# Latent attention: three rounded products of leads and rests for the projections and scores of three head pairs, and key scales spread by two

## The reference, cut to what matters

```python
def mla(c_q, c_kv, k_rope, ...):                       # 8 heads of 64 + 32 dimensions
    q = (rms_norm(c_q, q_a_g) @ w_uq).reshape(B, L, MLA_HEADS, QK_DIM)
    kv = (rms_norm(c_kv, kv_a_g) @ w_ukv).reshape(B, L, MLA_HEADS, NOPE_DIM + V_DIM)
    k = jnp.concatenate([k_nope, k_r], axis=-1)
    q = rms_norm(q, q_norm_g); k = rms_norm(k, k_norm_g)
    ...                                                # rotation of the last 32 dimensions
    o = causal_block_attention(q, k, v)                # softmax(q k^T * scale), causal, times v
    return o.reshape(B, L, MLA_HEADS * V_DIM) @ w_proj
```

## Time and profile before

| | |
|---|---|
| median of 3 runs | 2690.19 us (2686.73 to 2700.15) |
| profiled execution | 2695.79 us, of it span 2693.9 us |
| granted TensorE clock, mean | 0.987 |
| PE busy | 2615.2 us (97%) |
| DVE, ACT, POOL busy | 59%, 41%, 39% |

### The profile page before, as it was taken

One profiled execution on the slowest core, in us unless ns is written; L12 is line 12 of the kernel. 1 busy time (PEld: TensorE's weight loads), 2 busy tenths in 40 slices (PEclk: granted clock), 3 DMA queues, 4 the chain that ended last, 5 costly groups with the idle time before them and its releaser, 6 DMA issues.

```text
span 2693.9 us, 44428 instructions
## 1 busy us (share of the span) xinstructions
PE 2615.2 (97%) x16872; PEld 2318.6 (86%) x16872; DVE 1582.4 (59%) x2486; ACT 1101.7 (41%) x1841; POOL 1052.8 (39%) x675
## 2 busy tenths in 40 slices
PE   7998999999899999999999999999999999999998
PEld 5787788888699998888999999989987777788898
DVE  5665323324489885444476664599884453676665
ACT  4445423323432433433345543323324343454554
POOL 2121444444534222112456544443321124565564
PEclk9999999999999999989999999999999999999999
DMA  5221233232222111101322321222111112332222
GB/s 154 69 80 35 90 101 97 94 93 93 79 72 92 61 58 59 38 26 54 126 87 95 110 95 52 91 92 79 57 55 57 32 40 79 125 104 94 93 102 87
DMA packets 61761, 215.31 MB, mean 80 GB/s; under 512 B 8144, under 2 KB 8144, under 8 KB 61584
## 3 DMA queue, kind: packets, MB, share of 16 engines
q1 hardware_dynamic: 48128, 169.43, 19.8%
q10 hardware_dynamic: 13088, 42.18, 4.7%
q0 software_dynamic: 368, 1.23, 0.2%
HBM read 210.65 MB, written 2.16 MB: 79 GB/s over the span
## 4 chain that ended last, share of the span: by engine, by line
PE 62%; issue 11%; DVE 10%; POOL 5%; POOLq 5%; DVEq 4%; ACT 2%; DMA 0%; ACTq 0%; SPq 0%
PE ps L730 15%; PE ps L731 15%; PE ps L732 15%; POOLq L621 5%; POOL dl L634 3%; PE ps L1186 2%; DVE arena L2021 2%; PE ps L973 1%; PE ps L974 1%; PE ps L975 1%; PE ps L709 1%; PE ps L1161 1%; PE ps L837 1%; POOL wl L619 1%; DVE HID L2021 1%
## 5 line engine op out<-in xcount | busy, mean ns | idle before, releaser
L619 POOL TENSOR_TENSOR wl<-stage,wh 128x512 fp32r<-128x512 f32 (+1 forms) x470 | 807.1, 1731 | 1513.0 <-ACT wh L1326 1512.0
L730 PE MATMUL ps<-Uh,wh 128*128 128x264 f32 (+1 forms) x2624 | 884.7, 337 | 14.1 <-DVE Ul L2027 3.9
L731 PE MATMUL ps<-Ul,wh 128*128 128x264 f32 (+1 forms) x2624 | 854.5, 326 | 0.0
L732 PE MATMUL ps<-Uh,wl 128*128 128x264 f32 (+1 forms) x2624 | 852.8, 325 | 0.0
L1326 ACT ACTIVATE wh<-stage 128x1024 fp32r<-128x1024 f32 x314 | 332.7, 1060 | 835.8 <-PE ps L732 827.4
L730 PEld LDWEIGHTS ps<-Uh,wh 128*128 128x128 f32 x2624 | 497.9, 190 | 71.7 <-issue 17.2
L731 PEld LDWEIGHTS ps<-Ul,wh 128*128 128x128 f32 x2624 | 498.1, 190 | 40.2 <-issue 3.6
L732 PEld LDWEIGHTS ps<-Uh,wl 128*128 128x128 f32 x2624 | 496.2, 189 | 41.3
L2644 DVE SCALAR_TENSOR_TENSOR ps<-arena,v,ps 128x528 f32<-128x528 f32 x232 | 167.8, 769 | 8.3
L634 POOL TENSOR_TENSOR dl<-dstage,dh 128x512 fp32r<-128x512 f32 x112 | 144.6, 1310 | 48.5 <-ACT dh L1422 46.5
L731 PE MATMUL ps<-HIDl,wh 128*128 128x512 f32 (+1 forms) x384 | 137.5, 358 | 0.0
(11 more groups left out here) (377 smaller groups left out, 4926.9 us busy)
## 6 DMA issues: line engine op xcount, KB each, us to landing
stage<-w SPq DMA_DIRECT2D x318, 512.0 KB, 3.5
dstage<-w_down ACTq DMA_DIRECT2D x56, 512.0 KB, 4.3
arena<-bias_rows ACTq DMA_DIRECT2D x16, 448.0 KB, 5.0
arena<-w_mla ACTq DMA_DIRECT2D x8, 384.0 KB, 3.0
H<-xT SPq DMA_DIRECT2D x8, 256.0 KB, 6.9
out<-H ACTq DMA_DIRECT2D x8, 256.0 KB, 2.7
arena<-pT SPq DMA_DIRECT2D x1, 512.0 KB, 8.4
arena<-causal POOLq DMA_DIRECT2D x1, 320.0 KB, 3.9
```

The source lines that it names most:

```text
L619: rest = pool.tensor_tensor(dst[:, cols], stage[:, j, cols], lead[:, cols].bitcast(F32), ALU.subtract)
L730: pe.matmul(dst, w_lead, tok.part(a_lead, h), start=(k == 0), stop=False)
L731: pe.matmul(dst, w_lead, tok.part(a_rest, h), start=False, stop=False)
L732: mm = pe.matmul(dst, w_rest, tok.part(a_lead, h), start=False, stop=(k == len(acts) - 1))
```

## The change

For pairs 1, 2 and 3 the projections of queries and keys (`head_units`) and the scores (`split_score`) become split products. ScalarE writes the leads and VectorE the rests: of the two inputs of the projections once a layer (`low_leads`, `low_rests`), of the five weight tiles a pair (`weight_leads`, `weight_rests`), and of queries and keys a pair (`score_leads`, `score_rests`). For all four pairs the key scales are spread by two rounded products, from a diagonal of rounded scales and one of their rests, where one float32 product was; VectorE writes four diagonals in `head_inverses` where it wrote two. Pair 0 keeps float32 projections and scores, all pairs the values and squared sums. The rest is where things lie in memory.

```diff
-        diag_of = [W1[6], za[:, 1, :]]
+        rowsl = at("rowsl", [2, T], col_relu, F32R)
+        rowsz = at("rowsz", [2, T], col_za, F32R)
+        diagh = [at("diagh0", [T], col_arena + (KD + 6) * T, F32R), rowsz[:, 1, :]]
+        diagl = [rowsz[:, 0, :], rowsl[:, 0, :]]
+        qh_lead, kh_lead = [rowsl[:, 1 - hd, :] for hd in range(2)], [rowsz[:, hd, :] for hd in range(2)]
+        qh_rest, kh_rest = ([at(f"{name}{hd}", [T], col_arena + (KD + first + hd) * T, F32R) for hd in range(2)]
+                            for name, first in (("qh_rest", 0), ("kh_rest", 2)))
+        cq_lead, ckv_lead = at("cq_lead", [2, T], col_hid + 2 * EXPS, F32R), at("ckv_lead", [T], col_hid + 2 * EXPS + 2 * T, F32R)
+        cq_rest, ckv_rest = at("cq_rest", [2, T], col_arena + at_cq, F32R), at("ckv_rest", [T], col_arena + end_kraw - T, F32R)
+        ones_r = at("ones_r", [P], col_arena + end_state - P, F32R)
...
+                def split_score(hd, i):
+
+                    rows = slice(i * P, (i + 1) * P) if i < QT - 1 else slice(S, T)
+                    for half in range(1 if i < QT - 1 else 2):
+                        b = i % 2 if i < QT - 1 else half
+                        if i < QT - 1:
+                            dst, lead, rest = (x[:, 0:(i + 1) * P] for x in (ps[:, 4 + b, :], kh_lead[hd], kh_rest[hd]))
+                        else:
+                            dst, lead, rest = ps[0:META, 4 + b, 0:T2.width], T2.part(kh_lead[hd], half), T2.part(kh_rest[hd], half)
...
+                        pe.wait_ge(c_free[b], n.next(c_free[b]))
+                        pe.matmul(dst, qh_lead[hd][:, rows], lead, start=True, stop=False)
+                        pe.matmul(dst, qh_lead[hd][:, rows], rest, start=False, stop=False)
+                        pe.matmul(dst, qh_rest[hd][:, rows], lead, start=False, stop=True).then_inc(c_done[b], 1)
...
-                        yield from unit_steps([ones[0:T2.rows, :]], [diag_of[hd][0:T2.rows]], T2)
+                        for _ in unit_steps([ones_r[0:T2.rows, :]] * 2, [diagh[hd][0:T2.rows], diagl[hd][0:T2.rows]], T2):
+                            pass
+                        yield
...
+                    if pair == 0:
+                        yield from unit_steps([tile(pair, 0), tile(pair, 1)], [cq[:, 0, :], cq[:, 1, :]], T2)
+                        yield from unit_steps([tile(pair, 4)], [ckv], T2)
+                        yield from unit_steps([tile(pair, 2), tile(pair, 3)], [cq[:, 0, :], cq[:, 1, :]], T2)
+                    else:
+                        pe.wait_ge(low_split, n.next(low_split, 2 if pair == 1 else 1))
+                        wt = [(mla_lead[j // 3][:, j % 3 * P:(j % 3 + 1) * P], mla_rest[pair % 2][:, j * P:(j + 1) * P]) for j in range(5)]
+                        low = [(cq_lead[:, k, :], cq_rest[:, k, :]) for k in range(2)]
+                        yield from split_steps(wt[0:2], low, T2)
+                        yield from split_steps(wt[4:5], [(ckv_lead, ckv_rest)], T2)
+                        yield from split_steps(wt[2:4], low, T2)
...
+                            if pair > 0 and i == 0:
+                                pe.wait_ge(low_split, n.next(low_split))
+                            if pair > 0:
+                                split_score(hd, i)
+                            else:
+                                causal_score(hd, i)
...
+                def low_leads():
+                    for dst, src in ((cq_lead, cq), (ckv_lead, ckv)):
+                        ins = act.activation(dst, src, ACT.Copy)
+                    ins.then_inc(low_lead, 1)
+
+                def weight_leads(pair):
+                    act.wait_ge(mlaw_in[pair % 2], n.next(mlaw_in[pair % 2], 16))
+                    for dst, first, last in ((mla_lead[0], 0, 3), (mla_lead[1], 3, 5)):
+                        ins = act.activation(dst, mlaw[pair % 2][:, first * P:last * P], ACT.Copy)
+                    ins.then_inc(low_lead, 1)
+
+                def score_leads():
+                    for hd in range(2):
+                        act.wait_ge(qk_ready, n.next(qk_ready))
+                        act.activation(kh_lead[hd], kh_of[hd], ACT.Copy)
+                        act.activation(qh_lead[hd], qh_of[hd], ACT.Copy).then_inc(low_lead, 1)
...
                     yield from head_units(0)
+                    low_leads()
                     yield from gate_unit(0)
                     yield from key_scales()
+                    n.next(qk_ready, 2)
+                    n.next(mlaw_in[0], 16)
                     for pair in range(4):
+                        if pair < 3:
+                            weight_leads(pair + 1)
...
+                            score_leads()
                         yield from gate_unit(0, pair < 3)
...
+                    dve.tensor_copy(kscale_r[0:T2.rows], kscale[0:T2.rows])
+                    dve.drain()
+                    dve.tensor_tensor(kscale_l[0:T2.rows], kscale[0:T2.rows], kscale_r[0:T2.rows].bitcast(F32), ALU.subtract)
+                    dve.drain()
                     for hd in range(2):
-                        dve.tensor_tensor(diag_of[hd][0:T2.rows].rearrange("p (i c) -> p i c", c=T2.rows),
-                                          ident[0:T2.rows, 0:T2.rows].unsqueeze(1).to_broadcast([T2.rows, T2_TILES, T2.rows]),
-                                          kscale[0:T2.rows, :, hd:hd + 1].to_broadcast([T2.rows, T2_TILES, T2.rows]), ALU.mult)
+                        for dst, part in ((diagh[hd], kscale_r.bitcast(F32)), (diagl[hd], kscale_l)):
+                            dve.tensor_tensor(dst[0:T2.rows].rearrange("p (i c) -> p i c", c=T2.rows),
+                                              ident[0:T2.rows, 0:T2.rows].unsqueeze(1).to_broadcast([T2.rows, T2_TILES, T2.rows]),
+                                              part[0:T2.rows, :, hd:hd + 1].to_broadcast([T2.rows, T2_TILES, T2.rows]), ALU.mult)
                     dve.drain().then_inc(inv_ready, 1)
...
+                def low_rests():
+                    dve.wait_ge(low_lead, n.next(low_lead))
+                    less(cq_rest, cq, cq_lead.bitcast(F32))
+                    less(ckv_rest, ckv, ckv_lead.bitcast(F32)).then_inc(low_split, 1)
+
+                def weight_rests(pair):
+                    dve.wait_ge(low_lead, n.next(low_lead))
+                    for lead, first, last in ((mla_lead[0], 0, 3), (mla_lead[1], 3, 5)):
+                        ins = less(mla_rest[pair % 2][:, first * P:last * P], mlaw[pair % 2][:, first * P:last * P], lead.bitcast(F32))
+                    ins.then_inc(low_split, 1)
+
+                def score_rests():
+                    for hd in range(2):
+                        dve.wait_ge(low_lead, n.next(low_lead))
+                        less(kh_rest[hd], kh_of[hd], kh_lead[hd].bitcast(F32))
+                        less(qh_rest[hd], qh_of[hd], qh_lead[hd].bitcast(F32)).then_inc(low_split, 1)
...
                     head_inverses()
+                    low_rests()
                     yield from idle(KD - 2)
                     yield from key_scales()
                     for pair in range(4):
                         take()
-                        yield from idle(KD + 3)
+                        yield from idle(KD)
+                        if pair < 3:
+                            weight_rests(pair + 1)
+                        yield from idle(3)
                         branch(2 * pair, 0, False)
                         yield
                         if pair < 3:
                         if pair < 3:
                             yield from key_scales()
                         take()
-                        yield from idle(KD)
+                        if pair < 3:
+                            yield
+                            score_rests()
+                        yield from idle(KD - (pair < 3))
```

More of the change, by code:

```diff
@@ L361, in program @@
         mlaw = [mlaw0, work2[:, 6:8, :].rearrange("p k t -> p (k t)")[:, 0:6 * P]]
+        mla_rest = [at(f"mla_rest{j}", [5 * P], col, F32R) for j, col in enumerate((col_arena + at_mlaw, col_work2 + 6 * T))]
+        mla_lead = [at("mla_lead0", [3 * P], col_za + 2 * T + QT * P, F32R), at("mla_lead1", [2 * P], col_work2 + 6 * T + 6 * P, F32R)]
+        assert QT * P + 3 * P <= 2 * T and 8 * P <= 2 * T
         lb_max, lb_sum = (few(4) for _ in range(2))
@@ L1278, in _ @@
                             fill(1)
-                            if hd == i == 0:
-                                pe.wait_ge(qk_ready, n.next(qk_ready, 2))
-                            causal_score(hd, i)
+                            if pair == hd == i == 0:
+                                pe.wait_ge(qk_ready, 2 + n.now(qk_ready))
+                                n.next(qk_ready, 8)
+                            if pair > 0 and i == 0:
[4 more added lines that the diff above has]
+                                causal_score(hd, i)
                     fill(FILL_BEFORE[pair == 3])
@@ L2810, in _ @@
```

(1 more changed line is left out.)

17 lines of the change are left out of this document (11 added, 6 removed).

## The result

| | before | after |
|---|---|---|
| median, in the first comparison (7 runs each) | 2690.59 us (2686.73 to 2700.15) | 2675.01 us (2673.74 to 2682.02) |
| profiled execution, its span | 2695.79, 2693.9 | 2675.01, 2673.1 |
| granted TensorE clock in it | 0.987 | 0.992 |

The medians are 15.6 us apart, 0.58%. The ratio on record for the comparison is 0.9926, 95% interval 0.9911 to 0.9941, which is 0.74% or some 20 us; so the size is known to a few us only. Either is more than the 9.8 us of the forecast, and the clock in the last row says where to look.

The account below looks back on a forecast made before the run. TensorE, busy 97% of the span, was taken to bound the kernel. Two layers of 5.1 us, less 0.4 of cover, made 9.8 off the 2690.2 median: 2680.4, said as 2680; range 2668 to 2695.

Parts of the forecast that it names:

- likeliest case: Whole kernel: 2676 to 2686 us after the change, given a chance of 0.5.
- the sum: Gains expected to reach the end over setups and turns 0 to 3 of both layers: 9.8 us in all.
- Prices on TensorE: Rounded products: 0.114 us for 128 columns, 0.121 for 264; a head of scores 0.72 less, 20.4 us if all arrives.
- Narrow rounded products are dear: Rival at the scores: a 128-column rounded product takes 0.23 us, costing 4 us, so 2684; no separate chance given.
- Key scales give nothing in a turn: Spread in turns: VectorE's 3.33 us train keeps the end, so TensorE's 0.83 us saving gains 0; setups gain 0.42 each.
- Rests of weights: VectorE ahead of head 1's fourth mask, turns 0 to 2: 0.86 us, making TensorE wait 0.3 to 0.4.
- The rival with POOL: Rests of weights meet POOL's work and take 2.2 us, 8 us lost, 2688; chance 0.22 with other VectorE delays.
- At most 0.32 is to be had up to the queries of head 1: ScalarE's last copy before the queries' squares limits the gain there; 0.3 us taken in turns 1 and 2.
- The cover of `head_inverses`: Two more diagonals and small operations, 1.7 us, fit VectorE's idle 2.00 us ahead of `causal_outputs`, leaving 0.3.
- the 0.4 for the layer: Second layer: shorter gate steps of 512 columns give 0.4 us less cover over five steps, subtracted once.
- turn 3, "2 x 0.72 = 1.44": Last turn of each layer, without rests of weights: both heads' score savings arrive in full, 1.44 us.
- Half-clock stretches: Rival on TensorE's clock: one more long stretch in each of six turns costs 31 us, 2711; slower, chance 0.08.

Follow-up runs that it names:

- e2: Kernel before with only the key scales' spread changed to two rounded products; projections and scores stay float32. Median 2697.45 us against 2697.78, ratio 0.9995.
- e9: Kernel after with leads and rests of weights moved to the end of the turn before, and the old spread; 2684.21 us against 2695.99 before, ratio 0.9953.
- e5: Kernel after with the old float32 spread of the key scales and its two diagonals; 2683.1 us against 2696.22 before, ratio 0.9952.
- e8: Kernel after with leads and rests of a pair's weights written at the end of the turn before (pair 1's in the setup); 2676.92 us, ratio 0.9935 to before.
- e4: Kernel before with only the scores of pairs 1 to 3 as three rounded products; median 2681.66 us against 2697.78, ratio 0.9942.
- e6: Kernel after with useless rounded products repeated in each turn, to restore the turn lengths of before; 2691.97 us against 2696.22 before, ratio 0.9992.
- e7: Kernel before with 13 useless products in each of turns 0 to 2 of layer 1; 2694.35 us against 2696.22 before, ratio 0.9993.
- e1: The kernel before run again unchanged, as a measure of noise; median 2697.55 us against 2697.78, ratio 0.9998.

## Why the prediction was right, step by step

The forecast's range held, and 2675.0 lies 1 us below its likeliest case. The change's own work alone, 7.5 us by lengths or 8.8 by the fit, gives 2682 to 2683. The rest, some 7 to 8 us of the 15.6, is clock, and the sum had none; that the measured gain is of the forecast's order owes as much to the clock as to the sum.

- **Prices on TensorE** held: 0.28 us for three narrow rounded products (0.34 forecast) and 0.32 at head 1, 0.12 one of 264 columns, 6.27 us for a head of scores. "Narrow rounded products are dear" is out. The row behind 0.114 had been misread: its 20 instructions in 2.28 us are 10 float32 products of 48 columns, so that this price came out right by luck.
- **Key scales give nothing in a turn** held: the same 3.33 us train, TensorE waiting in front of its end, and e2 and e9 with the turn unchanged. In the setups the 0.42 shows as 0.4, but `ones_r` takes 0.27 of it back ahead of the squared sums; the sum had no term for that copy. The spread is worth 0.3 us in the kernel after by lengths, for 0.84 forecast. Equal clock gives 1.4 (e5), 1.9 (e9 against e8) and -2.0 (e2), which says more of the fit than of the spread.
- **Rests of weights** at the low price: 0.90 us for 0.86, the mask at 5.34 us for 5.43, TensorE waiting 0.34 for 0.3 to 0.4. The rival with POOL is out: the rests end at 1130.64 and POOL's next piece starts at 1130.92, all six pairs of rests of weights take 0.90 at most and each rest of queries or keys 0.70, and none of them overlaps a piece of POOL. So the rests didn't put the rule of the Trainium skill that the prediction weighed (SBUF — State Buffer, "SBUF: two separate sides") to the test. The `branch` in e2 agrees with it: it has two SBUF inputs, starts 0.06 us behind POOL's piece and takes 1.75 us for 0.69. A delay by POOL can so hit VectorE's train, only not where I had put it.
- **"At most 0.32 is to be had up to the queries of head 1"** was a limit of this order and not of the queries. ScalarE's copy ahead of the squares had its end set by the masks in front of it: with them on time, as in e4 and e8, head 1's 0.7 arrive. In the kernel after it was 0.40 for the 0.3 taken.
- **The cover of `head_inverses`**: 0.3 us forecast to remain, 0.37 measured. In the setup of layer 2 VectorE waited 1.40 us for the spread behind the rests, but there TensorE ran at 1.2 GHz for 3.4 us; in e6, without that stretch, the scaled keys start as the rests end (2048.59), so that the forecast's 0.7 us of cover were used up.
- **The sum.** Where no stretch disturbs both sides, lengths give: setup and turn 0 of layer 1 0.91 (forecast 0.92), turns 1 and 2 1.25 each (1.37), and in layer 2 0.72, 1.04 and 1.09 (before's undisturbed turns there from e7, after's start from e6; forecast 0.92, 1.37 and 1.37, less the 0.4 for the layer). The term that was most wrong is **turn 3, "2 x 0.72 = 1.44"**. Its head 0 gave its share, its head 1 did not. From head 1's first score to the first product with the values, in layer 2, before and after:

```profile
2203.98 0.38 PE L1161 MATMUL ps<-arena 128*128 128x128 f32 x2
...
2213.41 0.43 PE L1186 MATMUL ps<-arena 128*128 128x64 f32 x2 [0.72 <-ACT arena L576]
```

```profile
2182.97 0.30 PE L1187 MATMUL ps<-rowsz,rowsl 128*128 128x128 f32 x1
...
2192.24 0.43 PE L1220 MATMUL ps<-arena 128*128 128x64 f32 x2 [1.18 <-ACT arena L596]
```

  9.43 us became 9.27. The exponentials of the last score end when the masks and maxima let them, and TensorE's idle in front of the outputs grew from 0.72 to 1.18: 0.16 arrived where 0.72 was summed. The last turn of layer 2 is 0.85 shorter (55.85 to 55.00), and e8, with no rests in the way, is no shorter (55.02). I had read that chain of mask, maximum, exponential and copy for turns 1 and 2, and left it out for turn 3. In layer 1 it is 0.95 shorter. So turn 3 is 0.5 to 0.6 us a layer short of the 1.44. The lengths then sum to 8.0 us, less 0.54 for `ones_r` 7.5, for 9.8 forecast: 1.1 of the difference is turn 3, 0.5 `ones_r`, and the rest tenths in turns 0 to 2 that I haven't traced. The three parts alone give 0.2 + 2.5 + 7.0 = 9.7; together they give 7.5, and moving the rests of weights (e8) brings 1.7 of that back.
- **The clock.** Half-clock stretches were a rival with the wrong sign. The prediction allowed that they "can also be fewer" and named another count of them as what would prove the sum wrong; there is another count. The two profiled executions can be added up without the fit: three stretches of 10.2 us and one of 6.8 that are gone make 16.5 us less, two of 3.4 that are new 3 us more, and own work 7.5 less: 21.0 in all, and their spans differ by 20.8. The Trainium skill's advice against idle gaps (TensorE: Matmul & The Clock Gate, "Why this matters for your kernels") can't have decided: turns 0 to 2 of the kernel after have new waits and no stretch in its trace. The stretches of the attention begin 2.5 to 4 us behind the start of squared sums in these traces, all but one (3.4 us at 2139.7 in e2, behind the wait of 2.15). That doesn't say why one execution or one turn has the stretch and the next not.

What is shown and what is argued: that the profiled executions differ by own work and by stretches at 1.2 GHz is shown, to 0.2 us. That the kernel after has the higher clock as a kernel rests on seven executions, six of them at 0.992 or 0.993, where the 83 of before have 0.983 to 0.991; and that work put into its turns lowers it, on e6, whose twelve all have 0.990 or less. That the moment of the squared sums is the cause is argued from single traces, and e1 shows that it is not the only one; what else decides stays open. The first comparison's 15.6 us are fewer than the 20 between the kernel after and the 71 later executions of before, and the kernel after was run in the first comparison alone. So the clock's part was 7 to 8 us there and 11 to 12 against the later ones.

## What to carry to other kernels

When work on a bounding engine gets shorter, follow each part to the next wait for another engine: of 20.4 us saved on TensorE some 8 came through, and a chain found in one turn has to be looked for in the last turn too. Look for the small preparations too: a copy of 128 columns, 0.27 us late, took away more than half of the 0.4 that the spread gave a setup. Work of another engine that is put in front of a mask or a copy sets its end; moved to where that engine waits, it gave 0.4 us a turn back. Look at the granted clock beside every time, since it moved times by some 7 us between kernels here, and executions of one kernel lay up to 17 us apart; measure a stage by the distance of two like places, which repeated to 0.03 us where no stretch lay between; and don't keep a shift for its clock alone, since what decides it isn't known.

## What the runs showed of the hardware

- In the latent attention TensorE is at half its clock for 3.4 to 10.2 us behind squared sums (products of 48 columns) though busy for all of the time, in some turns and not in others with the same instructions, and in different turns in two executions of one program. A stretch of 10.2 us cost 4.52 us and one of 6.8 us 2.99 (47.90 less 44.91).
- Work added to a kernel can be hidden by its clock: e7 has 4.7 us more than before and took no longer (ratio 0.9980 to 1.0007; 4.0 us more at equal clock).
- A rounded product of 128 columns takes nearly as long as one of 264 (0.09 to 0.11 and 0.12 us), one of 384 0.17 and one of 512 0.23.
- On VectorE, a copy of 128 columns into the rounded format took 1.29 us (`ones_r`, both layers), a rest of 528 columns 0.70.
